# Decoder layer on one core: the Delta rule's inverse from 32-row blocks in place of 64-row blocks

## What is computed

```
lower = where(tri_strict, (k*beta) @ k.T * decay, 0) + eye
sol = triangular_solve(lower, [v*beta, k*beta*exp(gcum)])
u = u0 - wk @ s
o = (q*exp(gcum)) @ s + attn @ u
s = s * exp(g_last) + k_dec.T @ u
```

## Time and profile before

| | us |
|---|---|
| median of 3 runs | 1904.97 |
| lowest, highest | 1900.44, 1912.78 |
| the profiled execution | 1913.64 |
| its span, first to last instruction | 1912.0 |

### The profile page before, as it was taken

One profiled execution on the slowest core, in us unless ns is written; L12 is line 12 of the kernel. 1 busy time (PEld: TensorE's weight loads), 2 busy tenths in 40 slices (PEclk: granted clock), 3 DMA queues, 4 the chain that ended last, 5 costly groups with the idle time before them and its releaser, 6 DMA issues.

```text
span 1912.0 us, 33797 instructions
## 1 busy us (share of the span) xinstructions
PE 1817.2 (95%) x13392; PEld 1758.3 (92%) x13392; DVE 855.8 (45%) x1515; ACT 531.9 (28%) x1016; POOL 392.8 (21%) x194
## 2 busy tenths in 40 slices
PE   7999999999989999999999879999999999999995
PEld 7999999999978888888999769999999999999994
DVE  3003346674535667655561354442134441144437
ACT  3123334444312333331220353331112221022211
POOL 2121111111111010111221242222222222222314
PEclk9999999999979999999999889999999999999997
DMA  4111112242535455334451001111111111111111
GB/s 168 44 44 43 41 64 75 83 174 85 209 123 175 153 194 197 131 136 173 172 193 47 22 23 44 44 52 48 44 45 49 50 44 45 44 52 47 49 53 78
DMA packets 68091, 170.04 MB, mean 89 GB/s; under 512 B 9320, under 2 KB 38152, under 8 KB 66704
## 3 DMA queue, kind: packets, MB, share of 16 engines
q1 hardware_dynamic: 67280, 167.81, 25.6%
q10 hardware_dynamic: 720, 0.92, 0.1%
HBM read 138.32 MB, written 57.79 MB: 103 GB/s over the span
## 4 chain that ended last, share of the span: by engine, by line
PE 85%; DVE 9%; DMA 2%; issue 2%; ACT 2%; POOL 1%; POOLq 0%; SPq 0%; DVEq 0%; ACTq 0%
PE U L708 60%; PE U L812 7%; PE U L1167 3%; PE B L708 2%; PE B L798 1%; PE B L773 1%; PE B L975 1%; DMA stage<-in_wu 1%; PE B L998 1%; PE B L790 1%; DVE stats L1925 1%; DVE X L1797 1%; PE B L1115 1%; DVE og L1650 1%; DVE XTh L1714 0%
## 5 line engine op out<-in xcount | busy, mean ns | idle before, releaser
L626 POOL TENSOR_TENSOR wl<-stage,wh 128x1024 fp32r<-128x1024 f32 x127 | 309.7, 2438 | 1131.1 <-ACT wh L1188 1131.1
L708 PE MATMUL U<-xh,wh 128*128 128x344 f32 x1368 | 444.2, 325 | 0.2 <-ACT qkv L1192 0.2
L708 PE MATMUL U<-xl,wh 128*128 128x344 f32 x1368 | 437.8, 320 | 0.0
L708 PE MATMUL U<-xh,wl 128*128 128x344 f32 x1368 | 437.7, 320 | 0.0
L708 PE MATMUL U<-hh,wh 128*128 128x344 f32 x1056 | 338.6, 321 | 4.5 <-POOL hl L679 4.5
L708 PE MATMUL U<-hl,wh 128*128 128x344 f32 x1056 | 338.0, 320 | 0.0
L708 PE MATMUL U<-hh,wl 128*128 128x344 f32 x1056 | 337.3, 319 | 0.0
L708 PEld LDWEIGHTS U<-xh,wh 128*128 128x128 f32 x1368 | 258.0, 189 | 0.8 <-ACT qkv L1192 0.5
L708 PEld LDWEIGHTS U<-xh,wl 128*128 128x128 f32 x1368 | 257.8, 188 | 0.0
L708 PEld LDWEIGHTS U<-xl,wh 128*128 128x128 f32 x1368 | 257.7, 188 | 0.0
L708 PEld LDWEIGHTS U<-hh,wh 128*128 128x128 f32 x1056 | 199.2, 189 | 4.6 <-issue 4.6
(11 more groups left out here) (348 smaller groups left out, 2515.3 us busy)
## 6 DMA issues: line engine op xcount, KB each, us to landing
stage<-in_wu SPq DMA_DIRECT2D x126, 512.0 KB, 3.3
out_shift<-in_cache SPq DMA_DIRECT2D x8, 2046.0 KB
gate_scr<-gth SPq DMA_DIRECT2D x16, 516.0 KB, 3.0
gates<-gate_scr SPq DMA_DIRECT2D x8, 1032.0 KB, 5.0
out_shift<-in_cache SPq DMA_DIRECT2D x8, 1022.0 KB
dn_scr<-thb SPq DMA_DIRECT2D x12, 512.0 KB, 2.6
qkv<-in_xT SPq DMA_DIRECT2D x4, 1032.0 KB, 10.5
kvc<-in_cache SPq DMA_DIRECT2D x4, 1024.0 KB, 8.7
```

The lines of the kernel that those rows point to most:

```text
L626: nc.gpsimd.tensor_tensor(wl[:, par, :], stage[:, par, :], wh[:, par, :].bitcast(F32), ALU.subtract).then_inc(w_lo, 1)
L708: ins = nc.tensor.matmul(dst, a[:, par, w], b[:, xk, third(j)], start=first and n == 0 and m == 0, stop=last and n == len(ks) - 1 and m == 2)
```

## The change

The inverse is started from 32-row blocks. `LTq`, `XTq`, `X`, `Y` and `Lb` hold four quarters of 32 rows, 32 columns for each head, so that each is [128, 4, 32] where it was [128, 4, 64]. The first four levels (to 32 rows) make 16 products of 32x32 each time, four of them on the array's diagonal in turn, where there were 8. Level 4 joins 32 to 64 rows with a new block `Lo32`: 8 products, then 4 and 8. Level 5 joins 64 to 128 rows as before, but reads `Xw`, `Yw` and `XTf`, which have to be put together first: VectorE copies the off-diagonal blocks out of PSUM, ScalarE the diagonal ones, six copies in level 4, in place of the two at the tile's end. `xt_diag` counts two steps in a tile. There is no Lb for level 4, so one mask at L1787 goes away. The masks in `dcst` become smaller; XT and Xw are zeroed once. The number of f32 products in a tile goes from 136 to 236.

```diff
@@ -167,8 +168,9 @@
                 ATm = held(part, "ATm", [P, 2, 4 * P])
                 us, XT, S = (held(part, n, [P, 4 * P]) for n in ("us", "XT", "S"))
 
-                LTh, XTh, Loff, X, Y = (held(part, n, [P, 4, HB]) for n in ("LTh", "XTh", "Loff", "X", "Y"))
-                Lb = [held(part, f"Lb{n}", [P, 4, HB]) for n in range(2)]
+                Xw, Loff, Yw = (held(part, n, [P, 4, HB]) for n in ("Xw", "Loff", "Yw"))
+                LTq, XTq, Lo32, X, Y = (held(part, n, [P, 4, QB]) for n in ("LTq", "XTq", "Lo32", "X", "Y"))
+                Lb = [held(part, f"Lb{n}", [P, 4, QB]) for n in range(2)]
                 gT = held(part, "gT", [DN_H * TILES, P])
 
                 four = lambda ap: ap.rearrange("p (h k) -> p h k", h=4)
...
@@ -362,11 +364,13 @@
 
         LO, HI = slice(0, HB), slice(HB, P)
 
-        def half_blocks():
+        QUARTER = [slice(n * QB, (n + 1) * QB) for n in range(4)]
+
+        def quarter_blocks(which=range(4)):
 
             for h in range(DN_H):
-                for r in (LO, HI):
-                    yield h, r, slice(h * HB, (h + 1) * HB)
+                for n in which:
+                    yield h, n, QUARTER[n], slice(h * QB, (h + 1) * QB)
 
         QUARTERS = 18
         LEVELS = 6
...
@@ -906,7 +910,7 @@
             def updates(t):
                 pe.wait_ge(r_ready, t + 1)
                 pe.wait_ge(xt_ready, (t + 1) * (LEVELS + 1))
-                pe.wait_ge(xt_diag, t + 1)
+                pe.wait_ge(xt_diag, (t + 1) * 2)
                 for h, c in heads:
                     ins = nc.tensor.matmul(B34[:, 0, c], XT[:, c], us[:, c], start=True, stop=True)
                 ins.then_inc(u_done, 1)
...
@@ -958,8 +962,8 @@
                 beside.run(f_mask)
                 pe.wait_ge(xt_ready, i * (LEVELS + 1) + 1)
                 pe.wait_ge(squared, i * 2 + 2)
-                for h, r, c in half_blocks():
-                    ins = nc.tensor.matmul(B56[r, 0, c], XTh[r, h, :], ident[r, r], start=True, stop=True)
+                for h, n, r, c in quarter_blocks():
+                    ins = nc.tensor.matmul(B56[r, 0, c], XTq[r, h, :], ident[r, r], start=True, stop=True)
                 ins.then_inc(x_done, 1)
                 beside.run(f_x)
 
...
@@ -970,13 +974,18 @@
                         pe.wait_ge(side_ready, i * 3 + 1)
                     else:
                         pe.wait_ge(x_added, i * (LEVELS - 1) + lv)
-                    if lv < LEVELS - 1:
-                        for h, r, c in half_blocks():
+                    if lv < LEVELS - 2:
+                        for h, n, r, c in quarter_blocks():
                             ins = nc.tensor.matmul(B56[r, 1, c], Lb[(lv + 1) % 2][r, h, :], X[r, h, :], start=True,
                                                    stop=True)
+                    elif lv == LEVELS - 2:
+                        for h, n, r, c in quarter_blocks((0, 2)):
+                            ins = nc.tensor.matmul(B56[QUARTER[n + 1], 1, c], Lo32[r, h, :], X[r, h, :], start=True,
+                                                   stop=True)
                     else:
+                        pe.wait_ge(xt_diag, i * 2 + 1)
                         for h in range(DN_H):
-                            ins = nc.tensor.matmul(B56[HI, 1, h * HB:(h + 1) * HB], Loff[LO, h, :], X[LO, h, :],
+                            ins = nc.tensor.matmul(B56[HI, 1, h * HB:(h + 1) * HB], Loff[LO, h, :], Xw[LO, h, :],
                                                    start=True, stop=True)
                     ins.then_inc(y_done, 1)
                     if i > 0 and lv in (1, 3, 4):
...
@@ -993,15 +1002,21 @@
                     pe.wait_ge(xt_ready, i * (LEVELS + 1) + (lv + 1))
                     if lv == 0:
                         pe.wait_ge(side_ready, i * 3 + 2)
-                    if lv < LEVELS - 1:
-                        for h, r, c in half_blocks():
-                            ins = nc.tensor.matmul(B56[r, 0, c], XTh[r, h, :], Y[r, h, :], start=True, stop=True)
+                    if lv < LEVELS - 2:
+                        for h, n, r, c in quarter_blocks():
+                            ins = nc.tensor.matmul(B56[r, 0, c], XTq[r, h, :], Y[r, h, :], start=True, stop=True)
                         ins.then_inc(z_done, 1)
-                        for h, r, c in half_blocks():
-                            ins = nc.tensor.matmul(B7[r, c], Y[r, h, :], XTh[r, h, :], start=True, stop=True)
+                        for h, n, r, c in quarter_blocks():
+                            ins = nc.tensor.matmul(B7[r, c], Y[r, h, :], XTq[r, h, :], start=True, stop=True)
+                    elif lv == LEVELS - 2:
+                        for h, n, r, c in quarter_blocks((1,)):
+                            ins = nc.tensor.matmul(B56[r, 0, c], XTq[r, h, :], Y[r, h, :], start=True, stop=True)
+                        ins.then_inc(z_done, 1)
+                        for h, n, r, c in quarter_blocks((1, 3)):
+                            ins = nc.tensor.matmul(B7[QUARTER[n - 1], c], Y[r, h, :], XTq[r, h, :], start=True, stop=True)
                     else:
                         for h in range(DN_H):
-                            ins = nc.tensor.matmul(B7[LO, h * HB:(h + 1) * HB], Y[HI, h, :], XTh[HI, h, :],
+                            ins = nc.tensor.matmul(B7[LO, h * HB:(h + 1) * HB], Yw[HI, h, :], XTf[HI, h, HB:P],
                                                    start=True, stop=True)
                     ins.then_inc(zt_done, 1)
                 beside.rest()
...
@@ -1368,12 +1383,26 @@
                 beside.run(f_keys)
                 beside.run(f_mask)
                 act.wait_ge(x_done, i + 1)
-                nc.scalar.activation(X[:], four(B56[:, 0, 0:4 * HB]), ACT.Copy).then_inc(x_taken, 1)
+                nc.scalar.activation(X[:], four(B56[:, 0, 0:4 * QB]), ACT.Copy).then_inc(x_taken, 1)
                 beside.run(f_x)
                 for lv in range(LEVELS):
                     act.wait_ge(y_done, i * LEVELS + (lv + 1))
-                    rows = slice(0, P) if lv < LEVELS - 1 else HI
-                    nc.scalar.activation(Y[rows], four(B56[rows, 1, 0:4 * HB]), ACT.Copy).then_inc(y_taken, 1)
+                    if lv < LEVELS - 1:
+                        nc.scalar.activation(Y[:], four(B56[:, 1, 0:4 * QB]), ACT.Copy).then_inc(y_taken, 1)
+                    else:
+                        nc.scalar.activation(Yw[HI], four(B56[HI, 1, 0:4 * HB]), ACT.Copy).then_inc(y_taken, 1)
+                    if lv == LEVELS - 2:
+                        act.wait_ge(x_added, i * (LEVELS - 1) + lv)
+                        act.wait_ge(xt_ready, i * (LEVELS + 1) + (lv + 1))
+                        after(act, u_done, i)
+                        for n in range(2):
+                            nc.scalar.activation(Xw[QUARTER[n], :, n * QB:(n + 1) * QB], X[QUARTER[n]], ACT.Copy)
+                        for n in (2, 3):
+                            ins = nc.scalar.activation(XTf[QUARTER[n], :, n * QB:(n + 1) * QB], XTq[QUARTER[n]], ACT.Copy)
+                        ins.then_inc(xt_diag, 1)
+                        for n in (0, 1):
+                            ins = nc.scalar.activation(XTf[QUARTER[n], :, n * QB:(n + 1) * QB], XTq[QUARTER[n]], ACT.Copy)
+                        ins.then_inc(xt_diag, 1)
                     if i > 0 and lv == 1:
                         decayed_out(i - 1)
                     if i > 0 and lv == 3:
...
@@ -1386,10 +1415,6 @@
                         decay_of(i + 1)
                 if i > 0:
                     out_squares(i - 1)
-                act.wait_ge(xt_ready, i * (LEVELS + 1) + LEVELS)
-                after(act, u_done, i)
-                nc.scalar.activation(XTf[LO, :, 0:HB], XTh[LO], ACT.Copy)
-                nc.scalar.activation(XTf[HI, :, HB:P], XTh[HI], ACT.Copy).then_inc(xt_diag, 1)
                 act.wait_ge(ao_done, i + 1)
                 nc.scalar.activation(oh[:, 0:2, i * P:(i + 1) * P], B34[:, 0, 0:256].rearrange(
                     "p (n k) -> p n k", n=2), ACT.Copy).then_inc(ao_high, 1)
...
@@ -1667,7 +1692,8 @@
             st.link(nc.vector.tensor_copy(cf[:, 0, 0:32], B7[:, 0:32]))
             nc.vector.tensor_tensor(cf[:, 3, 0:32], B7[:, 32:64], cf[:, 0, 0:32], ALU.subtract).then_inc(cf_dve, 1)
             nc.vector.tensor_scalar(cf[:, 4, 0:32], cf[:, 0, 0:32], -1.0, None, ALU.mult).then_inc(cf_dve, 1)
-            nc.vector.memset(XTf[HI, :, 0:HB], 0.0)
+            nc.vector.memset(XT[:], 0.0)
+            nc.vector.memset(Xw[LO], 0.0)
             nc.vector.memset(S[:], 0.0).then_inc(s_ready, 1)
             dve.wait_ge(cf_act, 3)
             dve.wait_ge(dcst_in, 16)
...
@@ -1709,16 +1735,20 @@
                 nc.vector.tensor_tensor(Ew[:], ET[:], per_head(small(4)), ALU.mult).then_inc(decay_weighted, 1)
                 dve.wait_ge(decay_weighted, t + 1)
                 dve.wait_ge(front_done, t * 4 + 4)
```

(36 more changed lines are left out.)

13 lines of the change are left out of this document (6 added, 7 removed).

## The result

The changed kernel takes 1930.97 us (median of 4 runs, 1926.98 to 1936.77), the kernel before 1906.51 us beside it (1900.44 to 1912.78). The ratio is 1.0123, 95% interval 1.0098 to 1.0147: slower by 1.2%. The prediction was 1925 us with 1882 to 1950.

The account below looks back on a forecast made before the run. TensorE, busy 95% of the span, was taken as the bound. Tile savings of -22 us, stalls +27.6, block-fetch interference +7 and clock +7.5 gave net +20 on 1904.97: 1925 us, range 1882 to 1950.

Parts of the forecast that it names:

- the stalls: Tiles 1 to 7: TensorE waits for an instruction block delayed by cache copies, 29.5 us together, +27.6 over before.
- the clock: Tiles 2 to 5: long stalls lower TensorE's granted clock, three drops, +7.5 us.
- levels 0 and 5: Level 0: Lo32's operations offset by savings; level 5: two XTf copies replace one addition; 0 us each.
- the sum of -2.63 us a tile: One tile from tile 2 on, without stalls: shorter products, copies and additions save 2.63 us; -22 us over all tiles.
- the second-order term: Level section: 256 instructions run in about one block's fetch time and qk_rows' load interferes; +1 us a tile, 7 us.
- it is there at +15: Each tile's block delayed by the copies becomes usable about 15 us after L954.
- the bracketed case: Tile 2: the block slips in ahead of the copies, making the stall 2.4 us; otherwise 4.1 or 5.8.
- 2.3 us after: At a block's end, TensorE goes on 2.3 us after the missing instruction block has moved.
- Never dry: Rival: TensorE's instruction buffer is deeper, or blocks get in between the copies; no stalls, 1883 us; chance 0.20.
- half dry: Rival: most stalls are 1 to 2 us or fall where TensorE waits for VectorE anyway; 1897 us; chance 0.15.
- no fourfold overlap: Rival: product records cost 25 to 32 ns whatever their size; 1935 to 1950 us; chance 0.15.
- VectorE takes over: Rival: VectorE's more numerous smaller operations limit the tile; below 70% busy there, so tenths; no chance given.

Follow-up runs that it names:

- experiment 1: Changed kernel with the 24 cache copies (L548) issued early, in the bulk weight loop before any tile: 1898.52 us (0.9958).
- experiment 3: Changed kernel with the cache copies issued later in each tile, behind the load of the next q and k: 1934.83 us (1.0135).
- experiment 4: Changed kernel with 256 already met waits, packed into 128 TensorE instructions, before L966 of tile 0: 1940.67 us, a single execution.
- experiment 5: Kernel before with 20 extra one-column products in each of the first five levels, 400 more instructions a tile: 1937.19 us (1.0166).
- experiment 12: Kernel before with cache copies early, out_low and amx behind level 0's additions, new S's addition ahead, and larger weight-unit fill: 1896.09 us (0.993).
- experiment 2: Kernel before with the cache copies issued early, in the bulk weight loop: 1904.3 us (0.9981).
- experiment 8: Changed kernel with cache copies early, VectorE's out_low and amx after level 0's additions, new S's addition before the XTf copies: 1884.73 us (0.9891).

## Why the prediction was right, and where its terms were off

The direction, the time and the mechanism hold, and experiments 1, 3, 4 and 5 show the mechanism by its cause: moving the copies moves the gaps, moving the count moves the gaps, and a higher count alone, in the old algorithm, brings gaps of the same kind. That 1931 lies so near to 1925 is partly luck: the stalls came out 5.3 us smaller than the sum had them and the clock some 2 us, levels 0 and 5 cost 3.3 us that it had left out, and the two profiled runs differ by 15.9 us where the medians differ by 24.5.

**The products: right.** A group of 32 records was estimated at 0.26 us and takes 0.27; level 2 was to be 2.15 us and is 2.16; L958 to L966 was 4.55 us in tile 4. By experiment 12 the sum of -2.63 us a tile is right, -22 in all, but only in a kernel in which VectorE's queue lets it through. The pair with early copies alone agrees with this: -22, 3.3 for levels 0 and 5 (below) and 6.2 of gaps leave -12.5, and the spans of experiments 1 and 2 differ by 11.8. The rule of the Trainium skill that spoke against it (TensorEngine Tiling (Array Packing), Instruction Overhead, some 60 cycles a matmul), read as a cost of every record one after the other, as the prediction did, doesn't agree with the trace: 0.27 us for 32 records is 8.5 ns each, side by side. Within one of the four array tiles a record comes every 34 ns (8 in 0.27 us). The 60 cycles of the Trainium skill's section, at 2.4 GHz, would be an estimated 25 ns, so as a floor for one array tile the rule isn't contradicted.

**Level 0 and level 5, both priced at nothing: off by 0.2 and 0.27 us.** From L966 to level 1's L979 is 4.83 us (682.16 to 686.99) where 4.64 was the earlier trace rows: VectorE's queue with Lo32's two operations weighs a little more than what was saved. L988 to L997 is 1.42 us where L979 to L988 was 1.15 (700.37 to 701.52): XTf's two copies do not cost what one addition did, and they stand ahead of the new S. In seven tiles that is 3.3 us. More important is what "what the faster products save here becomes idle time" led to: L979's idle time in level 0 grew from 0.61 us to 1.68, and in tiles 3 to 5 the clock fell 0.3 to 0.9 us after the end of it.

**The stalls: right in place, a little high in sum, loose in each.** Predicted were 34.6 us more than before, the second-order term included; measured are 30.9 less 1.6, so 29.3. Block ends were predicted at instruction 561, 333, 361, 389, 417, 445 and 473 of tiles 1 to 7. A gap lies at each of these places: in tiles 1 to 7 TensorE stopped after 30, 29, 11, 25, 6, 4 and 18 records of the group that it was in, each within one record of the count. The lengths:

| tile | 1 | 2 | 3 | 4 | 5 | 6 | 7 |
|---|---|---|---|---|---|---|---|
| predicted | 2.6 | 4.1 | 5.75 | 5.6 | 4.6 | 3.45 | 3.35 |
| first record to next, measured | 4.9 | 1.2 | 5.6 | 2.8 | 4.5 | 3.0 | 2.7 |

The step that failed is "it is there at +15" in every tile: in tile 4 the products go on at +12.4, in tile 1 at +16.0, as their blocks' packets start at +9.8 and +13.7, outside the 12.4 to 13.3 of the prediction. In tile 2 the bracketed case happened, the block slipped in ahead of the copies (+6.2) and the next one ran dry instead. Nor is "2.3 us after" the block exact: in tile 3 the block moved between 689.5 and 690 (its packet starts at 689.9) and work went on at 692.74; over the tiles' main gaps it is 2.3 to 2.8 us from the packet's start to the next record. The rule of the Trainium skill (Runtime: NRT & Kernel Launch, Instruction fetch mechanics), by which TensorE has room for 128 KiB of instructions and crossing into the next 16 KiB is mostly hidden, doesn't agree with the trace: experiment 5's added instructions would then have cost no gap.

**The clock: wrong in kind, its size not measured.** The prediction had three drops after stalls above 5 us, 7.5 us in all. There are seven stretches at half in tiles 1 to 7, 51 us together, one in every tile, and in tiles 3 to 5 they begin right after the 1.7 us idle time before L979, not behind the long stall. In tiles 6 and 7 the same idle time (1.66) brought no fall, and the stretch begins 0.2 and 0.9 us after the stall. Their cost is not to be read directly, since a part of each is idle anyway (in 687.3 to 697.5 TensorE is busy 4.76 us). By what is left over, it is 15.9 (spans) - 29.3 + 22 - 3.3 = 5.3 us, an estimate with the error of every other term in it. Only experiment 8 gives a price for a stretch, 0.2 to 1.2 us.

**Rivals.** "Never dry" and "half dry" fall with the 30.9 us of "issue"; "no fourfold overlap" with the 0.27 us group; "VectorE takes over" was priced as tenths by VectorE's busy share, and between experiments 1 and 8 its order was worth 13.8 us in medians. The share of an engine says nothing of the place of one operation in its queue.

**Left open.** Why 256 instructions are the unit, and how far ahead blocks are asked for, is inferred from counts, not seen. Which part of experiment 8's gain is the clock and which the waits was not taken apart, and the traces show only 6.7 us of that gain. Why an idle time of 1.66 us brought the clock down in four tiles of experiment 1 and not in two others is open.

## What to carry to other kernels

Count instructions as well as time: when a change turns few large products into many small ones, look for "issue" gaps inside runs of equal instructions, and at what moves on the DMA engines just then. Large copies that nobody waits for are not free, as they can hold up the blocks of instructions; put them where an engine runs few instructions in a long time. After such a change look at the engine that is next in the chain, here VectorE's order, since the gain stops at its queue and the idle time can cost clock on top (experiment 8: about 1 us in each of two tiles).

## What the runs showed of the hardware

- TensorE's instructions come in blocks of 16 KB, by the counts 256 instructions; queued copies of 3.3 MB kept a block away until 10 to 14 us after the tile's start in six of seven tiles, and the engine stood still for up to 5.4 us.
- TensorE went on 2.3 to 2.8 us after the packet of the missing block had started (main gaps of tiles 1 to 7).
- An instruction that holds two waits whose semaphores have long been reached took TensorE's queue at most 87 ns (11.1 us for 128 of them, experiment 4).
- Products in four 32x32 tiles of the array run together: 8.5 ns per record, 0.27 us for 32. Forty records of one column took 0.43 us in the same way (experiment 5).
- TensorE's granted clock was at half (1.2 GHz) after idle times of 1.66 to 1.68 us before L980 in four of six tiles of experiment 1, and behind gaps on "issue" of 1.35 to 2.22 us in experiment 8; it stayed at full (2.4 GHz) in experiment 8's tiles 3 to 7 up to 853.6 us, where the idle time was 0.58 us and the gaps at most 1.2 us.
